# The first tiles of a stage multiplied at the end of the stage before it, in a two-block transformer kernel

## The chip, the cores and the metric

One core of one Trainium2 chip. The metric is the device time of one execution in microseconds, the median of the runs. TensorE (PE) multiplies, VectorE (DVE), ScalarE (ACT) and GpSimd (POOL) do the elementwise work, SyncE (SP) issues the transfers.

## The reference, cut to what matters

The kernel computes two model blocks over 512 positions of width 1024 in float32. Block one is an attention and RWKV mixer and an FFN of width 4096; block two has two layers, each a mixer and an FFN of width 2816. Each mixer ends in a projection `@ w_out`. What surrounds the change, for block two:

```python
def conv_ffn(h, w_in, conv_w, conv_b, w_out):
    u = h @ w_in
    u = lax.conv_general_dilated(u, conv_w[:, None, :], window_strides=(1,),
                                 padding=[(CONV_WIDTH - 1, 0)],
                                 dimension_numbers=('NWC', 'WIO', 'NWC'),
                                 feature_group_count=u.shape[-1]) + conv_b
    g, v = jnp.split(u, 2, axis=-1)
    return (jax.nn.silu(g) * v) @ w_out
...
        h = rms_norm_2(x, attn_norm[layer])
        if layer % 2 == 0:
            x = x + even_mixer(h, cos, sin, ...)
        else:
            x = x + odd_mixer(h, cos, sin, ...)
        h = rms_norm_2(x, ffn_norm[layer])
        x = x + conv_ffn(h, ffn_w_in[layer], ffn_conv_w[layer], ffn_conv_b[layer], ffn_w_out[layer])
```

## The kernel before, in words

All activations lie transposed, features on the 128 partitions and the 512 positions along the free axis, in eight slices of 128 features. A product of width 1024 is made tile by tile: a weight tile is 1024 x 128, loaded as 8 slices of 128 x 128. To keep float32 precision weights and activations are each cut into an upper and a lower part, and `three_passes` (L321) multiplies upper by upper, upper by lower and lower by upper: 24 matmuls of 128x128 by 128x512 for a tile (L326, L327, L328), summed in one PSUM bank.

One list, `plan` (L278), holds all weight tiles of the program in their order. Tile s passes SP's load into `raw` (two buffers, L286), ScalarE's upper part `whi` (`split_hi`, L302, or in a loop L813), GpSimd's lower part `wlo` (`split_lo`, L315, with L313 as the instruction) and TensorE's use. There are four buffers of `whi` and `wlo` (CUT = 4). ScalarE and GpSimd work AHEAD = 2 tiles ahead of TensorE: while a stage multiplies its tile m they split m + 2. Thus a stage ends with the first two tiles of the next one already split, and the next two loaded. `w_lo` counts tiles split, `w_used` tiles multiplied, `free` and `conved` the PSUM banks given back.

A stage is one Block (L149): all five engines meet in a barrier at its end and start the next stage together; GpSimd first clears the semaphores of the stage before (L158). The stages that the change touches, in the order of the program:
- `ffn` of block one, run twice with half of the width each (ch 0 and ch 1). The first stores its result in `f`, the second adds to it. Ch 0 begins with a norm (`Post`), ch 1 with nothing: the inputs `hi`, `lo` are the same, so its first tiles can be multiplied at once.
- `project_out` (L717) of each layer of block two: eight tiles; for each, VectorE adds to `xT` (L772), ScalarE makes the upper part of the next input and a square, VectorE the lower part (L775) and the sum of squares `acc` (L781).
- `ffn` of each layer of block two. It begins with `Ready` (L461): TensorE sums `acc` over the partitions (L393, 4 matmuls), VectorE and ScalarE form the reciprocal root, TensorE multiplies tile 0, spreads the root over the partitions (L402), and goes on with tile 1. VectorE scales each finished bank by the root (L963), so the products don't wait for it.
- `project` (L630) with four tiles (inputs of an indexer), begun by `Ready`; GpSimd scales the results (L650), TensorE and VectorE rotate three of them (`RotateTiles`, L603 and L610 to L614).
- `project` with 18 tiles, which begins with the indexer's own matmuls (L2107, L2113) and in which VectorE searches the largest scores.

In an `ffn` the up tiles use banks 0 to 3, four a turn, and the down tiles banks 4 and 5.

## Time and profile before

| | us |
|---|---|
| median of 3 runs (lowest, highest) | 2361.53 (2360.04, 2362.3) |
| profiled execution | 2364.71 |
| its span | 2362.9 |
| PE busy | 2201.6 (93%) |
| PEld busy (weight loads, beside PE) | 1765.5 (75%) |
| DVE busy | 1211.5 (51%) |
| ACT busy | 834.4 (35%) |
| POOL busy | 986.8 (42%) |
| lower parts of the weights, POOL L313, 347 times | 793.0 |

The table tells which engine is full on average: TensorE. The rest must be read by stretches. A row of the timeline gives start, duration, engine, line, operation, the tile written and those read, and in brackets how long the engine had been idle and which instruction released it. A release by "PEq L151" is the barrier between two stages. A matmul's printed duration (0.39 us) is longer than the distance to the next one, since they overlap; tiles are therefore measured from start to start.

### The profile page before, as it was taken

How to read it: one execution, taken by the hardware profiler on the slowest of the kernel's cores; microseconds unless marked ns; L12 is line 12 of the kernel's file. 1: busy time of each engine (PE TensorE's matmuls, PEld its weight loads, DVE VectorE, ACT ScalarE, POOL GpSimd, SP SyncE). 2: the span in 40 equal slices, each digit the busy share in tenths (PEclk: the TensorE clock that was granted, in tenths of full speed). 3: DMA queues.
4: the chain of work that ended last, by engine and by line, in shares of the span. 5: the costliest groups of instructions: out<-in, count | busy, mean ns of one | idle time of the engine just before them, and what ended most of it. 6: DMA issues, size and time to landing. Idle time of an engine off the chain costs nothing. (4 is left out here: it accounts for less than half of the span.)

```text
span 2362.9 us, 35241 instructions
## 1 busy us (share of the span) xinstructions
PE 2201.6 (93%) x13241; PEld 1765.5 (75%) x13241; DVE 1211.5 (51%) x1881; ACT 834.4 (35%) x1321; POOL 986.8 (42%) x515
## 2 busy tenths in 40 slices
PE   6995998699999999899879999999899899999998
PEld 4674986588888888777657788888676557888887
DVE  3336534677604772332663577731397633777601
ACT  3443222433313332332353333322323553333322
POOL 5231211244543444365563344444365514444442
PEclk8997999899999999999999999999999999999999
DMA  4220001223332333233102233333332003233332
GB/s 131 54 66 22 4 26 47 72 84 94 107 98 80 99 96 107 76 82 88 36 1 63 80 97 98 91 96 98 86 84 77 1 10 95 84 98 89 91 103 90
DMA packets 347229, 177.23 MB, mean 75 GB/s; under 512 B 20852, under 2 KB 344303, under 8 KB 347119
## 3 DMA queue, kind: packets, MB, share of 16 engines
q1 hardware_dynamic: 346620, 175.60, 26.0%
q8 instruction: 75, 1.23, 0.2%
q14 instruction: 36, 0.29, 0.0%
q10 hardware_dynamic: 210, 0.08, 0.0%
q0 software_dynamic: 288, 0.03, 0.0%
HBM read 173.57 MB, written 2.11 MB: 74 GB/s over the span
## 5 line engine op out<-in xcount | busy, mean ns | idle before, releaser
L313 POOL TENSOR_TENSOR wlo<-raw,whi 128x1024 fp32r<-128x1024 f32 (+3 forms) x347 | 793.0, 2289 | 1103.8 <-ACT whi L816 609.8
L326 PE MATMUL banks<-xhi,whi 128*128 128x512 f32 x1688 | 672.4, 398 | 6.0 <-DVE cb L974 3.9
L327 PE MATMUL banks<-xlo,whi 128*128 128x512 f32 x1688 | 661.9, 392 | 0.0
L328 PE MATMUL banks<-xhi,wlo 128*128 128x512 f32 x1688 | 661.7, 392 | 0.0
L326 PEld LDWEIGHTS banks<-xhi,whi 128*128 128x128 f32 x1688 | 320.2, 190 | 82.7 <-issue 12.9
L327 PEld LDWEIGHTS banks<-xlo,whi 128*128 128x128 f32 x1688 | 320.1, 190 | 69.0 <-issue 3.6
L328 PEld LDWEIGHTS banks<-xhi,wlo 128*128 128x128 f32 x1688 | 319.8, 189 | 67.6
L903 ACT ACTIVATE cb<-banks,conv 128x512 f32<-128x512 f32 x152 | 117.9, 778 | 446.6 <-DVE banks L963 446.6
L816 ACT ACTIVATE whi<-raw 128x1024 fp32r<-128x1024 f32 (+1 forms) x208 | 203.6, 988 | 172.1 <-PE banks L328 78.2
L326 PE MATMUL banks<-ghi,whi 128*128 128x512 f32 x608 | 236.6, 389 | 0.3 <-DVE glo L984 0.3
L327 PE MATMUL banks<-glo,whi 128*128 128x512 f32 x608 | 236.5, 389 | 0.0
L328 PE MATMUL banks<-ghi,wlo 128*128 128x512 f32 x608 | 236.5, 389 | 0.0
L963 DVE TENSOR_TENSOR banks<-banks,rs 128x512 f32<-128x512 f32 x152 | 106.2, 700 | 183.8 <-PE banks L328 166.5
L982 DVE CAST ghi<-gv 128x512 f32 (+1 forms) x76 | 168.4, 2216 | 9.0
L309 ACT ACTIVATE whi<-raw 128x1024 fp32r<-128x1024 f32 (+3 forms) x139 | 134.0, 970 | 47.3 <-PE banks L328 19.1
L326 PEld LDWEIGHTS banks<-ghi,whi 128*128 128x128 f32 x608 | 114.1, 188 | 24.3 <-DVE glo L984 0.7
L328 PEld LDWEIGHTS banks<-ghi,wlo 128*128 128x128 f32 x608 | 114.1, 188 | 23.8
L327 PEld LDWEIGHTS banks<-glo,whi 128*128 128x128 f32 x608 | 114.1, 188 | 23.6
L974 DVE SCALAR_TENSOR_TENSOR cb<-banks,conv,cb 128x510 f32<-128x510 f32 x152 | 113.8, 749 | 18.3 <-DVE cb L972 0.3
L972 DVE SCALAR_TENSOR_TENSOR cb<-banks,conv,cb 128x511 f32<-128x511 f32 x152 | 112.6, 741 | 3.8 <-ACT cb L903 3.8
L1005 DVE TENSOR_TENSOR xT<-banks,xT 128x512 f32 x16 | 11.1, 692 | 191.6 <-PE banks L328 191.6
L1054 POOL TENSOR_SCALAR ex<-ex,mx 128x128 f32<-128x128 f32 (+3 forms) x80 | 87.9, 1112 | 48.5 <-DVE mx L1116 34.1
(453 smaller groups left out, 2587.1 us busy)
## 6 DMA issues: line engine op xcount, KB each, us to landing
raw<-in_ffn_w_in_dram SPq DMA_DIRECT2D x88, 512.0 KB, 3.9
raw<-in_w_ffn_up_dram SPq DMA_DIRECT2D x64, 512.0 KB, 4.1
raw<-in_w_ffn_down_dram SPq DMA_DIRECT2D x32, 512.0 KB, 3.8
raw<-in_ev_w_in_dram SPq DMA_DIRECT2D x25, 512.0 KB, 4.0
raw<-in_ffn_w_out_dram SPq DMA_DIRECT2D x32, 384.0 KB, 3.5
raw<-in_ffn_w_out_dram SPq DMA_DIRECT2D x32, 320.0 KB, 3.2
raw<-in_od_w_in_dram SPq DMA_DIRECT2D x20, 512.0 KB, 3.9
raw<-in_w_in_dram SPq DMA_DIRECT2D x16, 512.0 KB, 3.8
```

The costliest lines, as they stand in the source:

```text
L309: w_hi.by(act.activation(whi[s % CUT][:, 0:n, :], raw[s % RAW][:, 0:n, :], ACT.Copy))
L313: return pool.tensor_tensor(wlo[c][:, 0:n, :], raw[b][:, 0:n, :], whi[c][:, 0:n, :].bitcast(F32), ALU.subtract)
L326: pe.matmul(acc, whi[b][:, k, :], hi(k), start=first and k == 0, stop=False)
L327: pe.matmul(acc, whi[b][:, k, :], lo(k), start=False, stop=False)
L328: mm = pe.matmul(acc, wlo[b][:, k, :], hi(k), start=False, stop=last and k == n - 1)
L816: act.activation(whi[s % CUT][:, 0:n, :], raw[s % RAW][:, 0:n, :], ACT.Copy).then_inc(w_hi.h, 1)
L903: act.activation(cb[j][:, :], bank[j][:, :], ACT.Identity, scale=conv[:, 2, bass.ds(c, 1)], bias=conv[:, 3, bass.ds(c, 1)])\
L963: dve.tensor_tensor(bank[j % 4][:, :], bank[j % 4][:, :], rs, ALU.mult).then_inc(scaled.h, 1)
L972: chain(dve.scalar_tensor_tensor(cb[j][:, 1:S], bank[j][:, 0:S - 1], conv[:, 1, bass.ds(c, 1)], cb[j][:, 1:S], ALU.mult, ALU.add))
L974: dve.scalar_tensor_tensor(cb[j][:, 2:S], bank[j][:, 0:S - 2], conv[:, 0, bass.ds(c, 1)], cb[j][:, 2:S], ALU.mult, ALU.add).then_inc(conve ...
L982: dve.tensor_copy(ghi[:, i * 2 + q, :], gv[q][:, :]).then_inc(upper.h, 1)
L1054: ins = pool.tensor_scalar(ex[u % 4][:, g, 0:w], ex[u % 4][:, g, 0:w], mx[u % 4][:, 2, g:g + 1], None, ALU.mult)
```

## The change: what it does

Five pairs of neighbouring stages are involved. The stage ahead gets a parameter `ahead` and the stage behind a parameter `done`. With `ahead=2` TensorE multiplies, after its own last tile, the first two tiles of the next stage into banks 0 and 1, before it goes to the barrier; with `done=2` the next stage begins with its third tile. Ffn ch 0 to ch 1, both `project_out` of block two to their `ffn`, and the first `ffn` of block two to the four-tile `project` do so with two tiles, the four-tile `project` to the 18-tile one with one tile. In the stage behind, the spread of the root comes after tile 2 in place of tile 0. Where the tiles ahead need the activation's lower part, a new signal `lowered` on VectorE's writes orders them. ScalarE's, GpSimd's and SP's programs keep their order, except that in the four-tile `project` GpSimd splits three tiles before it waits for the root, where it split one. A parameter `before` and a signal `moved` that nothing used are gone.

```diff
     def project(n, dst, lead=None, side=None, post=None, done=0, ahead=0):
...
-        lag = lead.SPREAD if lead else 0
+        lag = max(lead.SPREAD, done) if lead else 0
...
             def _(pe):
+                aside, done_lag = 0, lag if lead and done else 0
...
-                    if m >= tiles_:
+                    if m >= max(tiles_, done):
                         pe.wait_ge(w_lo.h, s + 1)
...
-                    if lead and m == lead.SPREAD:
+                    if lead and m == lag:
                         lead.pe_spread(pe)
-                    if m >= 1:
-                        side.pe(pe, scaled, m - 1)
-                side.pe(pe, scaled, n - 1)
+                    while m > done_lag and aside < m - ahead:
+                        side.pe(pe, scaled, aside)
+                        aside += 1
+                for j in range(ahead):
+                    pe.wait_ge(w_lo.h, s0 + n + j + 1)
+                    pe.wait_ge(free.h, n - 3 + j)
+                    three_passes(pe, bank[j][:, :], (s0 + n + j) % CUT, KD, lambda k: hi[:, k, :], lambda k: lo[:, k, :], True, True)\
+                        .then_inc(w_used.h, 1)
+                while aside < n:
+                    side.pe(pe, scaled, aside)
+                    aside += 1
...
+    def project_out(oT, scale, mixed=None, make_side=None, ahead=0):
...
+                for j in range(ahead):
+                    pe.wait_ge(w_lo.h, s0 + n + j + 1)
+                    pe.wait_ge(free.h, n - 3 + j)
+                    three_passes(pe, bank[j][:, :], (s0 + n + j) % CUT, KD, lambda k: feed["hi"][:, k, :], lambda k: feed["lo"][:, k, :], True, True,
+                                 lowered).then_inc(w_used.h, 1)
...
+    def ffn(w_up, ff, w_down, conv, first, pairs, parts, func, add, acc_to, make_lead=None, tail=None, done=0, ahead=0):
...
                     lead.pe_sums(pe)
-                    up(0, False, 0, 1)
+                    up(0, False, done, done + 1)
                     lead.pe_spread(pe)
-                    up(0, False, 1)
+                    up(0, False, done + 1)
                 else:
-                    up(0, False)
+                    up(0, False, done)
...
+                for j in range(ahead):
+                    pe.wait_ge(w_lo.h, end + j + 1)
+                    three_passes(pe, bank[j][:, :], (end + j) % CUT, KD, lambda k: hi[:, k, :], lambda k: lo[:, k, :], True, True,
+                                 lowered if tail else None).then_inc(w_used.h, 1)
...
-                        project(4, lambda m: to[m], lead=Ready(c1),
+                        project(4, lambda m: to[m], lead=Ready(c1), done=2, ahead=1,
...
-                    project(18, lambda m: dsts[m],
+                    project(18, lambda m: dsts[m], done=1,
...
-                ("sums",) if ch == 1 else None)
+                ("sums",) if ch == 1 else None, done=2 * ch, ahead=2 - 2 * ch)
...
-                project_out(oT, ("ffn_norm", KD * layer))
+                project_out(oT, ("ffn_norm", KD * layer), ahead=2)
...
-                ("feed", "attn_norm", KD) if layer == 0 else ("last", "final_norm"))
+                ("feed", "attn_norm", KD) if layer == 0 else ("last", "final_norm"), done=2, ahead=2 - 2 * layer)
```

TensorE's program before, from the end of the first `project_out` of block two into its `ffn`. L151 is the jump to the barrier, `whi_12` the second weight buffer, and a name behind "waits" can be that of an earlier use of the semaphore:

```order
L328 MATMUL banks<-hi,wlo_15 128x512
L151 UNCONDITIONAL_BRANCH
L853 UNCONDITIONAL_BRANCH [waits barrier_Pool_Activation_PE_DVE_SP_release]
L393 MATMUL banks<-cst,acc 128x1 x4
L326 MATMUL banks<-xhi,whi_12 128x512 [waits w_lo_22]
...
L402 MATMUL banks<-cst,st 128x128 [waits sq_114]
L402 MATMUL banks<-cst,st 128x128 x3
L326 MATMUL banks<-xhi,whi_13 128x512 [waits w_lo_22]
```

Tile 0 follows the barrier and the sums, the spread (L402) stands between tile 0 and tile 1. The same place after the change (here exped_91 is `lowered` and flipped_93 is `free`):

```order
L328 MATMUL banks<-hi,wlo_15 128x512
L326 MATMUL banks<-xhi,whi_12 128x512 [waits exped_91,flipped_93,w_lo_22]
...
L326 MATMUL banks<-xhi,whi_13 128x512 [waits exped_91,flipped_93,w_lo_22]
...
L151 UNCONDITIONAL_BRANCH
L865 UNCONDITIONAL_BRANCH [waits barrier_Pool_Activation_PE_DVE_SP_release]
L393 MATMUL banks<-cst,acc 128x1 x4
L326 MATMUL banks<-xhi,whi_14 128x512 [waits w_lo_22]
...
L402 MATMUL banks<-cst,st 128x128 [waits summed_115]
L402 MATMUL banks<-cst,st 128x128 x3
L326 MATMUL banks<-xhi,whi_11 128x512 [waits w_lo_22]
```

The tiles in `whi_12` and `whi_13` now stand ahead of the barrier, and the first tile behind it is that in `whi_14`.

GpSimd's program after the change, from the end of ffn ch 0 into ch 1 (before, it reads the same, with x28 in the row of L158):

```order
L313 TENSOR_TENSOR wlo_15<-raw_9,whi_11 128x1024 [waits w_hi_21]
L313 TENSOR_TENSOR wlo_16<-raw_10,whi_12 128x1024 [waits w_hi_21]
L151 UNCONDITIONAL_BRANCH
L155 UNCONDITIONAL_BRANCH [waits barrier_Pool_Activation_PE_DVE_SP_gather]
L158 ISA x29
L835 UNCONDITIONAL_BRANCH
L835 ISA
L313 TENSOR_TENSOR wlo_17<-raw_9,whi_13 128x1024 [waits w_hi_21]
```

The tile in `wlo_17`, the new stage's third, is cut behind the barrier and behind the clearing of the semaphores, in both kernels.

TensorE's program after the change, at the end of the four-tile `project` (pre_109 is `scaled`):

```order
L603 MATMUL banks<-iq,sw 128x512 [waits flipped_93,pre_109]
L603 MATMUL banks<-iq,sw 128x512 [waits pre_109]
L326 MATMUL banks<-xhi,whi_12 128x512 [waits sg1_110,w_lo_22]
...
L603 MATMUL banks<-ik,sw 128x512 [waits pre_109]
L151 UNCONDITIONAL_BRANCH
L660 UNCONDITIONAL_BRANCH [waits barrier_Pool_Activation_PE_DVE_SP_release]
L2123 MATMUL banks<-cst,ciw 128x128 x4
```

Before, each of the three rotations stood behind one tile; now two stand together, the tile done ahead (`whi_12`) follows them, and the third rotation is the last before the barrier.

## Rows read from the trace of the kernel before

**Rows 1.** The page, 40 slices of the span: TensorE's busy share in tenths.
```profile
PE   6995998699999999899879999999899899999998
```

**Rows 2.** TensorE's waits, whole span: waiter, releaser, us in total, times, longest.
```profile
PE banks L393 <- PEq L151: 20.1, 6, 4.4
...
PE banks L326 <- DVE lo L559: 15.1, 3, 8.6
...
PE banks L326 <- DVE cb L974: 3.9, 1, 3.9
PE banks L326 <- POOL wlo L313: 3.1, 1, 3.1
```

**Rows 3.** The timeline at seam 2, project_out to ffn, block two's first layer.
```profile
1299.89 0.39 PE L328 MATMUL banks<-hi,wlo 128*128 128x512 f32 x1
1303.86 1.84 PE L393 MATMUL banks<-cst,acc 128*128 128x1 f32 x8 [3.58 <-PEq L151]
1305.03 4.69 POOL L313 TENSOR_TENSOR wlo<-raw,whi 128x1024 fp32r<-128x1024 f32 x2 [4.69 <-ACT whi L816]
1313.30 1.05 PE L402 MATMUL banks<-cst,st 128*128 128x128 f32 x8
1314.11 0.48 PE L326 MATMUL banks<-xhi,whi 128*128 128x512 f32 x1
...
1330.54 0.39 PE L326 MATMUL banks<-xhi,whi 128*128 128x512 f32 x1
```

**Rows 4.** The timeline of TensorE at seam 5, project_out to ffn, second layer.
```profile
1982.12 0.39 PE L328 MATMUL banks<-hi,wlo 128*128 128x512 f32 x1
...
2012.96 0.39 PE L326 MATMUL banks<-xhi,whi 128*128 128x512 f32 x1
```

**Rows 5.** The timeline at seam 1, ffn ch 0 to ch 1.
```profile
714.39 0.39 PE L328 MATMUL banks<-ghi,wlo 128*128 128x512 f32 x1
714.94 0.69 DVE L1007 COPY f<-banks 128x512 f32 x1 [10.19 <-PE banks L328]
715.96 0.47 PE L326 MATMUL banks<-xhi,whi 128*128 128x512 f32 x1 [1.18 <-PEq L151]
718.07 2.40 POOL L313 TENSOR_TENSOR wlo<-raw,whi 128x1024 fp32r<-128x1024 f32 x1 [10.54 <-ACT whi L816]
...
729.94 0.75 DVE L974 SCALAR_TENSOR_TENSOR cb<-banks,conv,cb 128x510 f32<-128x510 f32 x1
...
737.84 0.39 PE L326 MATMUL banks<-xhi,whi 128*128 128x512 f32 x1
```

**Rows 6.** The timeline at seams 3 and 4, around the four-tile projection.
```profile
1667.60 0.39 PE L328 MATMUL banks<-ghi,wlo 128*128 128x512 f32 x1
1671.43 1.33 PE L393 MATMUL banks<-cst,acc 128*128 128x1 f32 x8 [3.44 <-PEq L151]
1672.62 2.36 POOL L313 TENSOR_TENSOR wlo<-raw,whi 128x1024 fp32r<-128x1024 f32 x1 [5.21 <-ACT whi L309]
...
1700.10 1.02 PE L603 MATMUL banks<-ik,sw 128*128 128x512 f32 x2
1703.91 0.63 PE L2107 MATMUL banks<-cst,ciw 128*128 128x128 f32 x4 [2.79 <-PEq L151]
```

**Rows 7.** TensorE in four stretches: length, busy (x), clock, DMA share, GB/s.
```profile
391.90:398.70 6.80, 3.09 (x7) 0.51 0.19 59
419.30:422.70 3.40, 3.40 (x9) 0.50 0.53 155
470.50:477.20 6.70, 5.07 (x12) 0.50 0.00 0
1303.40:1310.10 6.70, 6.24 (x19) 0.50 0.17 50
```

**Rows 8.** The timeline at the end of the 18-tile projection.
```profile
1807.59 1.95 DVE L2196 SCALAR_TENSOR_TENSOR ckv<-ckv,pcol,part 128x512 f32<-128x512 f32 x1
...
1817.83 2.84 PE L2229 MATMUL banks<-ckv,ukp 128*128 128x512 f32 x4 [2.32 <-PEq L151]
```

More of the change, by code:

```diff
@@ L628, in in_turn, with project @@
                     mm.then_inc(w_used.h, 1)
-    def project(n, dst, lead=None, side=None, post=None, before=None):
+    def project(n, dst, lead=None, side=None, post=None, done=0, ahead=0):
         s0 = state["s"]
@@ L697, in _ @@
                     act.wait_ge(w_used.h, s0 + m + 1)
-                    if before:
-                        before(act, m)
                     free.by(act.activation(dst(m), bank[m % 4][:, :], ACT.Copy))
@@ L715, in project @@
         state["s"] += n
-    def project_out(oT, scale, mixed=None, make_side=None):
+    def project_out(oT, scale, mixed=None, make_side=None, ahead=0):
         s0, n = state["s"], KD
@@ L721, in project_out @@
         to = xT if mixed is None else mixed
-        free, moved, uppered, squared, summed = (sig(x) for x in ("free", "moved", "uppered", "squared", "summed"))
+        free, uppered, lowered, squared, summed = (sig(x) for x in ("free", "uppered", "lowered", "squared", "summed"))
         with ExitStack() as ctx:
@@ L775, in _ @@
                         dve.scalar_tensor_tensor(feed["lo"][:, m - 1, :], xT[:, m - 1, :], col(scale[0], scale[1] + m - 1),
-                                                 feed["hi"][:, m - 1, :].bitcast(F32), ALU.mult, ALU.subtract)
+                                                 feed["hi"][:, m - 1, :].bitcast(F32), ALU.mult, ALU.subtract).then_inc(lowered.h, 1)
                     if m >= 2:
@@ L782, in project_out @@
         state["s"] += n
-    def ffn(w_up, ff, w_down, conv, first, pairs, parts, func, add, acc_to, make_lead=None, tail=None):
+    def ffn(w_up, ff, w_down, conv, first, pairs, parts, func, add, acc_to, make_lead=None, tail=None, done=0, ahead=0):
         hi, lo, rs, acc = feed["hi"], feed["lo"], feed["rs"], feed["acc"]
@@ L797, in ffn @@
             scaled, uppered, squared, summed = (sig(n) for n in ("scaled", "uppered", "squared", "summed"))
-            taken = sig("taken")
+            taken, lowered = sig("taken"), sig("lowered")
             chain0 = dve_chain.n
@@ L1010, in _ @@
                                 dve.scalar_tensor_tensor(lo[:, m, :], xT[:, m, :], pcol[:, bass.ds(m + (vec[tail[1]] + tail[2]), 1)],
-                                                         hi[:, m, :].bitcast(F32), ALU.mult, ALU.subtract)
+                                                         hi[:, m, :].bitcast(F32), ALU.mult, ALU.subtract).then_inc(lowered.h, 1)
                             if tail:
```

## The prediction

> **What bounds the kernel now.** I read the slices of the page first, for where TensorE is not full; then the waits of TensorE; then the timeline at the five seams the change touches; last the granted clock around idle stretches. The slices show TensorE at nine tenths or more in most of the span [rows 1]: the 24 matmuls of a weight tile follow each other without a hole. Three tiles fill 1314.11 to 1330.54, that is (16.43 - 0.1)/3 = 5.44 us a tile, the 0.1 being the slower first matmul after a stop [rows 3]. So the time can only change at the holes. The waits [rows 2] show that holes come in two kinds: TensorE held at a stage's start ("PEq L151", the barrier), and TensorE held for a split weight or activation tile.
>
> The seams, each measured from the start of the last matmul of the old stage to the start of the fifth tile of the new one (so that four tiles are inside):
> - seam 2, first output projection of block two into its FFN: 1299.89 to 1330.54 = 30.65 us [rows 3]. Inside stand a barrier after VectorE's and ScalarE's tail (hole 3.58), the sums, and a stretch at half clock.
> - seam 5, the same in the second layer: 1982.12 to 2012.96 = 30.84 us [rows 4].
> - seam 1, first FFN pass of block one into its second: 714.39 to 737.84 = 23.45 us [rows 5]; the hole is only 1.18 us and the four tiles (21.76) run at full clock.
> - seams 3 and 4, FFN into the four-tile projection and that into the 18-tile one: from 1667.60 to the first matmul of the 18-tile stage at 1703.91 = 36.31 us [rows 6].
>
> **What is added and what it waits for.** The extra tiles are the ones whose weights are already split, since ScalarE and GpSimd work two tiles ahead (AHEAD). Nobody works further ahead than before: the split of the third tile (index 2) still stands in the new stage, behind the barrier. Before, two tiles (10.88 us) ran over that split; now TensorE arrives at it at once. What it costs is in the rows: at seam 2 GpSimd starts at 1305.03, when ScalarE has done its half of the split, and needs 4.69/2 = 2.35 us for a tile, so tile 2 is ready 3.5 us after the stage's start (1303.86) [rows 3]. At seam 3 it is 1672.62 + 2.36 - 1671.43 = 3.55 [rows 6]. At seam 1 GpSimd starts only at 718.07, 2.11 us in: it clears 28 semaphores first (29 after the change); ready at 720.47, 4.5 us in [rows 5]. So the change hides a hole that was made by the old stage's tail and opens one made by the new stage's head, and the sum is the difference.
>
> The barrier with TensorE last: at seam 1 VectorE started 0.55 us after the start of the last matmul, and TensorE 0.33 us after VectorE's end (715.63 to 715.96) [rows 5]; 0.88 together. That is worked out from one seam; 0.6 to 1.2 would shift the total by about 1 us either way.
>
> Each seam after, from the same start, c being what the clock costs:
> - seam 2: two tiles 10.88, barrier 0.88, split 3.5 + 0.1 for the signal (the sums, 1.0 us, lie beside it), tile 2 5.54, the spread 0.81 (1313.30 to 1314.11 [rows 3]), tile 3 5.54 = 27.25 + c. Against 30.65: -3.4 + c.
> - seam 5: the same 27.25 + c against 30.84: -3.6 + c.
> - seam 1: 10.88 + 0.88 + 4.5 + 0.1 + 10.98 = 27.35 + c against 23.45: +3.9 + c. Here there was nothing to win but 1.2 us, and a wait of 4.5 us is put in.
> - seams 3 and 4: 10.88 + 0.88 + 3.55 + 0.1 + 5.54 + 0.81 + 5.54, two rotation matmuls of 0.5 us each (half of the row of 1.02, which is two passes), the tile done ahead 5.6, then the third rotation matmul and from its start the 3.81 us that it took before (1700.10 to 1703.91: VectorE's rotation is still behind it, uncovered [rows 6]) = 37.7 + c. The 18-tile stage then has one tile less, 5.54. So 32.2 + c against 36.31: -4.1 + c.
>
> Without c: +3.9 - 3.4 - 3.6 - 4.1 = -7.2 us.
>
> **The clock.** A TensorE that has stood still pays a second time. After the 3.1 us hole in block one's output projection the granted clock is 0.50 (1.2 GHz of 2.4) for 3.40 us of busy time, cost 1.7 us; after a 3.9 us hole 5.07 us busy, cost 2.5; after the 8.6 us hole 3.09 us busy, cost 1.5, the rest of the slow stretch having passed in the hole; at seam 2, hole and sums together, 6.24 us, cost 3.1 [rows 2, 7]. At seam 1 there is no slow stretch now: its 23.45 us are four tiles at 5.44 and the barrier [rows 5]. After the change seams 2, 3 and 5 have a hole of about 0.6 us, the sums (1.0) and a hole of 2.5: nearest is the 3.1 us hole, 1.7 each. (Of the old 3.1 I thus give back 1.4 at each; it is inside the -3.4, -3.6 and -4.1 already, since the 30.65, 30.84 and 36.31 hold the old slow stretches.) Seam 1 has a new hole of 5.2 us, between the 3.9 and the 8.6: 2.0. Together 3 x 1.7 + 2.0 = 7.1. Bounds of c: 0 at the low end, 3.4 at the high end (a slow stretch of 6.8 us with TensorE busy throughout).
>
> **Covers that I count at nothing.** The first tile done ahead reads as its last of eight slices the one that VectorE writes in the tail; the tail's whole hole is 3.58 us [rows 3], and that slice is asked for seven eighths into the tile, 4.8 us in. Banks 0 and 1 were freed long before. In the 18-tile stage ScalarE and GpSimd split tile 2 while tile 1 runs (5.44 us against the 3.5 that both engines took at seam 2 [rows 3]), a margin of nearly 2 us. VectorE begins tiles 0 and 1 no later than the new third tile ends; the fifth tile needs its bank back, and at seam 1 VectorE gives it at 729.94 + 0.75 = 730.69, 14.7 us into the stage [rows 5], while the new tile 3 ends 4.6 + 10.98 + c = 15.6 + c in: a thin cover of 0.9 us. VectorE's chain of the 18-tile stage ends at 1809.54 [rows 8] and the next stage starts at 1817.83, 0.33 us after all have arrived, so its slack is 8.0 us; these shrink by 5.5 to 2.5 [rows 8]. One semaphore more to clear is at most 2.11/28 = 0.08 us, at two stage starts.
>
> **Sum.** -7.2 + 7.1 = -0.1 us. The profiled execution would take 2364.7 us (span 2362.9 and 1.8 around it) less 0.1; the median of the runs lies 3.2 us below it, at 2361.5. I forecast 2361.4. A difference under 0.2% (4.7 us) can't be told from none here.
>
> **Rivals.**
> 1. The clock does not fall at the new holes of seams 2, 3 and 5: each is split by the sums into pieces of 0.6 and 2.5 us. Then only seam 1 pays: -7.2 + 2.0 = -5.2, 2356.3 us (2354.3 if it doesn't pay either). For it: the 1.18 us hole of seam 1 costs no clock today [rows 5]. Against it: a 3.1 us hole was followed by a slow stretch [rows 2, 7]. Chance 0.15. The Trainium skill (TensorE: Matmul & The Clock Gate, section "HAM oscillation — how this bites in real kernels") has a rule of thumb that only a wait above a certain length costs clock, and it sets that length above each of these pieces, so by it this rival would hold. The 3.1 us hole lies below that length too and was followed by the slow stretch, so the trace does not agree.
> 2. The clock falls for the whole long stretch at all four, c = 3.4: 13.6 - 7.2 = +6.4, 2367.9 us, slower. The place is seam 1 most of all, where +3.9 and 3.4 meet with nothing returned. It decides from a total c of 7.2 + 4.7 = 11.9 us on. For it: seams 2, 3 and 5 have the long stretch today, after holes no longer in total than the new ones. Chance 0.15.
> 3. Tile 2's weights are found split, and the holes close altogether: seam 2 becomes 10.88 + 0.88 + 1.0 + 5.44 + 0.81 + 5.44 = 24.45, -6.2; seam 5 -6.4; seams 3 and 4 -6.8 (37.7 less the 2.65 of waiting); seam 1 -0.8; together -20.2, 2341.3 us. Against it: ScalarE's and GpSimd's programs have the split of tile 2 behind the barrier as before. Chance 0.05.
> 4. VectorE's chain in the 18-tile stage becomes its end (its rotations wait in another order, or it stretches beside GpSimd): up to 5.5 of the 5.54 us of that tile are lost, 2367. Chance 0.05.
> The forecast with c between 1 and 2.9 a seam on average holds 0.60.
>
> **How the numbers follow.** Of the forecast's own 0.60, running from 2357 to 2366, nearly all is within 0.2%; some 0.05 falls out at the fast end and 0.02 at the slow end. Faster: 0.15 + 0.05 + 0.05 = 0.25. Slower: 0.12 of rival 2, 0.03 of rival 4 and 0.02 = 0.17. Same: 0.58. The range for 8 in 10 goes from 2354.5, at rival 1, to 2367.
>
> **What would show it.** Right: the barrier waits before the sums at seams 2, 3, 5 fall from about 3.5 to under 1 us, and new waits of TensorE for "POOL wlo" appear, 2.5 us at three seams and about 4.5 at seam 1, where a stretch at clock 0.5 is new; seam 4's 2.79 us hole stays. Wrong: no wait for "POOL wlo" at the stage starts (rival 3), or full clock behind them (rival 1).

## The result and the profile after

The changed kernel takes 2369.55 us (median of 6, 2367.58 to 2374.07) beside 2361.41 for the kernel before (6 runs, 2356.8 to 2362.3): ratio 1.0033, interval 1.0022 to 1.0043. It is slower by 8.1 us, more than the 4.7 us that can be told from no change. The forecast was 2361.4 and the range ended at 2367.0; both missed. A second comparison on another chip gave 2374.07 beside 2365.3, ratio 1.0037 (1.0022 to 1.0052).

In all that follows a "cut" is the making of the upper part (ScalarE) or the lower part (GpSimd, L313) of a weight tile, a "hole" is a stretch in which TensorE runs nothing, and a "slow stretch" is one in which its granted clock is at half. TensorE's waits in the changed kernel, whole span (waiter, releaser, us in total, times, longest); lines behind L313 have moved on by up to 16:

```profile
PE banks L326 <- POOL wlo L313: 16.0, 6, 4.9
...
PE banks L393 <- PEq L151: 11.5, 6, 5.4
...
PE banks L2245 <- PEq L151: 4.2, 1, 4.2
...
PE banks L2123 <- PEq L151: 2.5, 1, 2.5
```

Beside [rows 2]: the waits for the barrier ahead of the sums fell from 20.1 us to 11.5, and those for a cut tile rose from 3.1 us, once, to 16.0, six times. The four new waits for a cut are 12.6 us together, where the forecast had 2.5 us at three seams and about 4.5 at seam 1. The timeline at seam 1, all engines (start, duration, engine, line, operation, tiles, in brackets the idle time before and its releaser):

```profile
725.27 0.39 PE L328 MATMUL banks<-xhi,wlo 128*128 128x512 f32 x1
725.98 1.30 DVE L979 TENSOR_TENSOR banks<-banks,rs 128x512 f32<-128x512 f32 x2 [10.36 <-PEq L151]
726.03 2.00 ACT L828 ACTIVATE whi<-raw 128x1024 fp32r<-128x1024 f32 x2 [20.97 <-PEq L151]
728.17 4.66 POOL L313 TENSOR_TENSOR wlo<-raw,whi 128x1024 fp32r<-128x1024 f32 x2 [20.64 <-ACT whi L828]
...
730.56 0.80 PE L326 MATMUL banks<-xhi,whi 128*128 128x512 f32 x1 [4.90 <-POOL wlo L313]
```

GpSimd starts its cut 2.2 us into the stage and TensorE stands until the first of the two is done. The hole is 4.90 us where it was 1.18 [rows 5]. At seam 2 and at seam 5, TensorE alone:

```profile
1317.44 0.39 PE L328 MATMUL banks<-xhi,wlo 128*128 128x512 f32 x1
1318.15 1.02 PE L393 MATMUL banks<-cst,acc 128*128 128x1 f32 x8 [0.32 <-PEq L151]
1321.72 0.80 PE L326 MATMUL banks<-xhi,whi 128*128 128x512 f32 x1 [2.54 <-POOL wlo L313]
...
1329.91 1.05 PE L402 MATMUL banks<-cst,st 128*128 128x128 f32 x8
```
```profile
2004.08 0.80 PE L326 MATMUL banks<-xhi,whi 128*128 128x512 f32 x1 [2.54 <-POOL wlo L313]
```

The hole of 3.58 us ahead of the sums (the same at both seams before, [rows 3] show the first) is down to 0.32 at both, and one of 2.54 stands behind them. Its first matmul takes 0.80 us where one at full clock takes 0.48. The granted clock at these places, where 0.50 is 1.2 GHz of 2.4 (stretch, length, TensorE busy and its instructions, clock, DMA share, GB/s), in the order seam 1, seam 2, seam 3, behind the 18-tile stage, seam 5:

```profile
730.00:736.80 6.80, 6.24 (x15) 0.50 0.54 154
1320.50:1327.30 6.80, 5.58 (x13) 0.50 0.52 152
1689.10:1692.50 3.40, 3.40 (x9) 0.50 0.67 182
1822.20:1829.00 6.80, 5.38 (x7) 0.50 0.00 0
2003.10:2009.90 6.80, 5.83 (x14) 0.50 0.53 154
```

**The 18-tile stage.** It begins at 1712.79 and its successor at 1823.62, 110.83 us; before it was 1817.83 - 1703.91 = 113.92 [rows 6, 8]. It has one tile (5.54) less and is only 3.1 us shorter. Its end, TensorE and then VectorE:

```profile
1819.00 0.39 PE L328 MATMUL banks<-xhi,wlo 128*128 128x512 f32 x1
1823.62 2.05 PE L2245 MATMUL banks<-ckv,ukp 128*128 128x512 f32 x2 [4.24 <-PEq L151]
```
```profile
1818.94 3.35 DVE L2211 RECIPROCAL part<-sq 128x512 f32<-128x512 f32 x1
1822.33 0.75 DVE L2212 SCALAR_TENSOR_TENSOR ckv<-ckv,pcol,part 128x512 f32<-128x512 f32 x1
```

VectorE now ends last, at 1823.08, and TensorE waits 4.24 us where it waited 2.32. From the stage's first matmul VectorE's chain took 1809.54 - 1703.91 = 105.63 us before and 1823.08 - 1712.79 = 110.29 now. A large part of the difference is one group near its start, three additions of a 128x128 mask. In the kernel before, VectorE and GpSimd:

```profile
1713.90 2.70 DVE L2159 TENSOR_TENSOR score<-score,future 128x128 f32<-128x128 f32 x3
```
```profile
1713.54 2.50 POOL L313 TENSOR_TENSOR wlo<-raw,whi 128x1024 fp32r<-128x1024 f32 x1 [11.30 <-ACT whi L309]
1718.28 1.30 POOL L650 TENSOR_TENSOR cq<-cq,rs 128x512 f32<-128x512 f32 x1 [2.24 <-ACT cq L700]
```

and in the changed one:

```profile
1723.11 5.99 DVE L2175 TENSOR_TENSOR score<-score,future 128x128 f32<-128x128 f32 x3
1729.13 1.48 DVE L2183 MAX8 top<-score 128x8 f32<-128x256 f32 x3
```
```profile
1722.44 2.82 POOL L313 TENSOR_TENSOR wlo<-raw,whi 128x1024 fp32r<-128x1024 f32 x1 [17.47 <-ACT whi L309]
1725.23 1.34 POOL L650 TENSOR_TENSOR cq<-cq,rs 128x512 f32<-128x512 f32 x1
1726.52 2.43 POOL L313 TENSOR_TENSOR wlo<-raw,whi 128x1024 fp32r<-128x1024 f32 x1
1728.91 1.34 POOL L650 TENSOR_TENSOR cq<-cq,rs 128x512 f32<-128x512 f32 x1
```

Before, one GpSimd operation lay over the additions and they ended 0.56 us after it (1716.60 beside 1716.04). Now three GpSimd operations follow each other without a pause, and the additions end 0.15 us after the third (1729.10 beside 1728.95). Taken one by one, the three additions end at 1725.41, 1726.71 and 1729.10, and the three GpSimd operations at 1725.26, 1726.57 and 1728.95: each addition ends 0.14 or 0.15 us behind one of them. Before, the first waited in the same way (to 1716.20) and the other two took 0.28 us each. The order changed because tile 0's product is there from the start: its scaling (L650) stands ready at once, between the cuts, where it used to come later.

The same happens further on. VectorE rotates the first tiles of the stage (L610, L611, L614), and L614, which takes 0.69 us when it is alone, took 2.70 where it began beside a cut. For tile 0, before and after:

```profile
1729.87 0.69 DVE L614 TENSOR_TENSOR cq<-cq,rotated 128x512 f32<-128x512 f32 x1
```
```profile
1742.37 2.70 DVE L614 TENSOR_TENSOR cq<-cq,rotated 128x512 f32<-128x512 f32 x1
```

Which of these operations meet a cut differs between the two kernels, and the changed one meets more of them.

**Where the time stands.** TensorE's line cut at holes that every profile has, in us; the second column is a new profile of the kernel before (run b1_before_again below), the last the forecast's difference:

| from, to (times of the first profile) | before | before again | changed | forecast |
|---|---|---|---|---|
| 472.1 to 977.4, holds seam 1 | 505.23 | 505.24 | 511.92 | +5.9 |
| 1254.9 to 1703.9, holds seams 2 and 3 | 449.03 | 447.44 | 451.24 | +1.4 |
| 1703.9 to 1817.8, the 18-tile stage | 113.92 | 113.97 | 110.83 | -5.5 |
| 1817.8 to 1936.1 | 118.28 | 118.23 | 119.27 | 0 |
| 1936.1 to 2350.4, holds seam 5 | 414.29 | 412.91 | 413.33 | -1.9 |
| rest of the span, not touched | 762.2 | 763.8 | 761.8 | 0 |

A second profile of the changed kernel (run a1_changed_again) has 511.85, 451.16, 110.84, 119.28 and 413.28, all within 0.1 us of the first, and 765.7 in the rest: between these two executions only what the change leaves alone moved, by 4 us.

The +1.4 is seam 2's -1.7 and, for seams 3 and 4 with the tile done ahead still in, 37.7 + 1.7 - 36.31 = +3.1.

### The profile page after: what moved, and what is told of

Same layout as the page of the kernel before. It is cut to its first block and busy times, and to the rows that moved or that the text cites. A ratio compares the mean times of both kernels' runs of the same rounds, so it can differ in the third digit from the quotient of the medians.

```text
span 2368.4 us, 35252 instructions
## 1 busy us (share of the span) xinstructions
PE 2203.7 (93%) x13241; PEld 1764.7 (75%) x13241; DVE 1210.5 (51%) x1881; ACT 834.4 (35%) x1321; POOL 985.9 (42%) x515
## 5 line engine op out<-in xcount | busy, mean ns | idle before, releaser
L313 POOL TENSOR_TENSOR wlo<-raw,whi 128x1024 fp32r<-128x1024 f32 (+3 forms) x347 | 793.1, 2290 | 1125.0 <-ACT whi L828 612.9
L326 PE MATMUL banks<-xhi,whi 128*128 128x512 f32 x1688 | 673.1, 399 | 17.4 <-POOL wlo L313 12.6
L988 DVE SCALAR_TENSOR_TENSOR cb<-banks,conv,cb 128x511 f32<-128x511 f32 x152 | 112.6, 741 | 12.6 <-ACT cb L919 12.6
```

The costliest lines, as they stand in the source:

```text
L313: return pool.tensor_tensor(wlo[c][:, 0:n, :], raw[b][:, 0:n, :], whi[c][:, 0:n, :].bitcast(F32), ALU.subtract)
L326: pe.matmul(acc, whi[b][:, k, :], hi(k), start=first and k == 0, stop=False)
L988: chain(dve.scalar_tensor_tensor(cb[j][:, 1:S], bank[j][:, 0:S - 1], conv[:, 1, bass.ds(c, 1)], cb[j][:, 1:S], ALU.mult, ALU.add))
```

## The experiments

Each is an edit of the changed kernel unless said otherwise. Ratios are to the kernel before, timed on the same chip; profile segments are against the table's first column.

**e1_seam1_only and e2_without_seam1: is it seam 1?**

```diff
 e1: tiles ahead at seam 1 alone
-    project_out(oT, ("ffn_norm", KD * layer), ahead=2)
+    project_out(oT, ("ffn_norm", KD * layer))
-    done=2, ahead=2 - 2 * layer)
+    )
-    project(4, ..., lead=Ready(c1), done=2, ahead=1,
+    project(4, ..., lead=Ready(c1),
-    project(18, ..., done=1,
+    project(18, ...,
 e2: everything but seam 1
-    done=2 * ch, ahead=2 - 2 * ch)
+    done=0, ahead=0)
```

> Only seam 1 (FFN ch 0 to ch 1) has its two tiles ahead; the other seams are as before. Theory (the change loses at seam 1: TensorE waits 4.9 us for GpSimd's cut of the third tile and then runs 6.8 us at half clock): in the profile the second FFN pass starts its fifth tile 6 to 7 us later than before, and all behind it is shifted by that; timed +5 to +7.5 us against before. Rival (seam 1 is neutral, the loss lies at the later seams): within 1 us of before.

Measured: 2370.58 (11 runs) beside 2364.48, ratio 1.0024 (1.0015 to 1.0033), 6.1 us slower, as expected; its segment with seam 1 is 5.64 longer. The fifth tile starts 5.2 us later than before (28.68 us for 23.45), not 6 to 7: the hole is 4.90 us again, but the slow stretch behind it is 3.4 us long in this profile, not 6.8.

> The changed kernel with seam 1 undone, seams 2 to 5 kept. Theory: the timed result falls by 6 to 7 us from the changed kernel's, to -1 to +2 us against before, since seams 2 and 5 return 1 us each, seam 3 with 4 returns 2.4 and gives 2.4 back in the 18-tile stage and 1 more by the clock. Rival (the loss of 8 us lies in seams 2 to 5): still +5 us or more.

Measured: 2366.14 (12 runs, one of them a stray 5605.41) beside 2364.48, ratio 1.0008 (1.0000 to 1.0017), 1.7 us. That is inside the expected -1 to +2, and the interval reaches 1.0000. So seam 1 carries most of the loss, and the other four together don't gain, where the forecast had them at -7.2 - 3.9 + 3 x 1.7 = -6.0.

**e3_without_seam4: what is the tile ahead at seam 4 worth?**

```diff
-    project(4, ..., lead=Ready(c1), done=2, ahead=1,
+    project(4, ..., lead=Ready(c1), done=2,
-    project(18, ..., done=1,
+    project(18, ...,
```

> The changed kernel without the one tile ahead at seam 4 (four-tile projection to 18-tile one). Theory (VectorE's chain ends the 18-tile stage once TensorE has one tile less): the hole at that stage's end falls from 4.2 to 2.3 us, the half-clock stretch behind it from 6.8 to 3.4 us, and the time does not rise though a tile of work goes back: -1 us against the changed kernel, so +4 to +7 against before. Rival (TensorE's chain ends the stage in both): the tile ahead is worth its cover, and without it the kernel is 2 us slower or more than the changed one.

Measured: 2373.87 (5 runs) beside 2364.48, ratio 1.0042 (1.0029 to 1.0055). The hole at the end of the 18-tile stage is 2.32 us and the slow stretch behind it 3.4, as expected, but the gain did not come: the kernel is 9.4 us over before, where the changed one is 8.1 and 8.8 over. That is less than the 2 us of the rival too, and the intervals overlap. What ate the gain stands at the other end of the stage. TensorE at the end of the four-tile stage:

```profile
1706.80 0.59 PE L603 MATMUL banks<-ik,sw 128*128 128x512 f32 x1
1713.09 1.09 PE L2123 MATMUL banks<-cst,ciw 128*128 128x128 f32 x4 [5.70 <-PEq L151]
```

With two tiles gone to the stage before and none put in, nothing is left to multiply beside the rotations, and the hole is 5.70 us against 2.79 [rows 6] and 2.45 with the tile. The clock is at half for 6.8 us after it, and the 18-tile stage takes 114.68.

**e4_mask_early: take VectorE's additions out of GpSimd's way.**

```diff
+                if x == 8:
+                    dve.wait_ge(self.got.h, 80)
+                    dve.wait_ge(self.added.h, 9)
+                    for t, _ in tiles_:
+                        y = self.score[:, t - 1, t * P:(t + 1) * P]
+                        ins = dve.tensor_tensor(y, y, self.future, ALU.add)
+                    chain(ins)
...
-            dve.wait_ge(self.got.h, 80)
             dve.wait_ge(self.added.h, len(self.order))
-            for n, _ in tiles_:
-                x = self.score[:, n - 1, n * P:(n + 1) * P]
-                ins = dve.tensor_tensor(x, x, self.future, ALU.add)
-            chain(ins)
```

> The changed kernel, with VectorE's three additions of the mask (128x128 each) in the 18-tile stage moved ahead of GpSimd's first cut of that stage. Theory (they took 5.99 us in place of 2.70 because GpSimd's cuts, now back to back, hold what both engines share): the three additions take under 1.5 us in all, VectorE's chain ends 2.5 to 4 us earlier, the hole at the stage's end falls to 2.3 to 3 us, and the kernel gains 1.5 to 3 us on the changed one. Rival (the additions are late because TensorE's first matmuls ran at half clock): they still take 5 us or more wherever they stand, and nothing is gained.

Measured: 2369.76 (10 runs) beside 2364.48, ratio 1.0021 (1.0012 to 1.0031): 5.3 us over before where the changed kernel is 8.1 and 8.8 over, which fits the expected 1.5 to 3, though the intervals overlap. VectorE, its last operation of the chain at the stage's end, and then GpSimd:

```profile
1724.81 0.70 DVE L2176 TENSOR_TENSOR score<-score,future 128x128 f32<-128x128 f32 x3
1725.54 4.42 DVE L2170 SCALAR_TENSOR_TENSOR score<-part,iwt,score 128x512 f32<-128x512 f32 x3
1730.00 1.48 DVE L2185 MAX8 top<-score 128x8 f32<-128x256 f32 x3
...
1816.14 1.80 DVE L2214 SCALAR_TENSOR_TENSOR ckv<-ckv,pcol,part 128x512 f32<-128x512 f32 x1
```
```profile
1726.62 2.79 POOL L313 TENSOR_TENSOR wlo<-raw,whi 128x1024 fp32r<-128x1024 f32 x1 [17.47 <-ACT whi L309]
1729.38 1.73 POOL L650 TENSOR_TENSOR cq<-cq,rs 128x512 f32<-128x512 f32 x1
```

Alone the three additions take 0.70 us, so 5.3 of the 5.99 were waiting. But the operations behind them (L2170, 2.46 us before) now meet the cut and take 4.42. The stage is 109.27 in place of 110.83 (its end hole is 2.32 again) and the slow stretch after it 3.4 us in place of 6.8. The meeting was moved, not removed. Yet the chain ends 1817.94 - 1716.97 = 100.97 us into the stage, 9.3 us sooner than in the changed kernel and not the expected 2.5 to 4, since with the additions moved the later operations fall elsewhere between GpSimd's and wait less (L611 and L614 together 12.6 us, 18.0 in the changed kernel). So the meetings set the chain's length, but what one of them costs can't be read from its own row. The rival (additions late because of the clock) is out: they took 0.70 us.

**a1_changed_again, e5_split_ahead, e6_split_and_mask, e8_seam1_split_ahead: cut further ahead as well.** In e5 ScalarE and GpSimd cut as many further tiles before the barrier as TensorE has multiplied ahead, so that the third tile is ready when the new stage starts. The core of the edit (in `project`; `project_out` and `ffn` likewise):

```diff
 GpSimd
-                    split_lo(pool, s0 + m + AHEAD)
+                    if m >= done:
+                        split_lo(pool, s0 + m + AHEAD)
...
+                for j in range(ahead):
+                    split_lo(pool, s0 + n + AHEAD + j)
 ScalarE
-                    if m >= AHEAD or not lead:
+                    if m >= AHEAD or not lead and m >= done:
                         split_hi(act, s0 + m + AHEAD)
...
+                for j in range(ahead):
+                    split_hi(act, s0 + n + AHEAD + j)
```

e6 is e5 with e4's edit, e8 is e5's for seam 1 alone and nothing ahead at the others.

> The changed kernel itself, on the same chip as the next three. It should come out 5 to 9 us slower than before, as in its first timing (8.1 us), and give the number that the others are held against.

> The changed kernel, with ScalarE's and GpSimd's cuts of as many further tiles as TensorE multiplies ahead moved in front of the barrier too, at all five seams (the four cut buffers suffice). Theory: the waits of TensorE for GpSimd's cut behind the barriers (4.9, 2.5, 2.6, 2.5 us) go, and with them the slow stretches there (3.0, 2.6, 1.6, 2.6 us), 20 to 22 us in all; 12 to 16 us faster than before. Rival (the cut buffers or ScalarE's place in its queue make TensorE wait elsewhere, or the clock falls anyhow at the barrier and the sums): the waits come back at the fifth tile or the slow stretches stay, and under half of it is gained, 2 to 5 us faster than before.

> The kernel with all cuts ahead, and VectorE's three mask additions ahead of GpSimd's first cut of the 18-tile stage. Theory: another 1 to 3 us on the one without it, since VectorE's chain no longer ends that stage: hole there 2.3 us in place of 4.2. Rival (VectorE's chain ends it still, since the stage before starts it in the same way): hole 4 us, no gain.

> Only seam 1 has its two tiles ahead, and there the cuts of the third and fourth tile stand ahead of the barrier as well; all else is as before. Theory: TensorE starts the third tile 0.7 to 1 us after its last matmul, no slow stretch follows, and the kernel is within 1.5 us of before, where the same seam without the cuts ahead cost 6 us. Rival (the tiles ahead cost by themselves, as through the loop's end or the bank's return): still 3 us or more slower than before.

Measured, beside 2365.3: a1 2374.07 (10 runs), 1.0037 (1.0022 to 1.0052); e5 2346.39 (6 runs), 0.9923 (0.9903 to 0.9942); e6 2346.63 (6 runs), 0.9924 (0.9906 to 0.9942); e8 2364.84 (12 runs), 1.0000 (0.9989 to 1.0011). Seam 1 and seam 2 in e5, TensorE:

```profile
726.37 0.39 PE L328 MATMUL banks<-xhi,wlo 128*128 128x512 f32 x1
...
727.08 0.47 PE L326 MATMUL banks<-xhi,whi 128*128 128x512 f32 x1 [0.33 <-PEq L151]
```
```profile
1311.96 0.39 PE L328 MATMUL banks<-xhi,wlo 128*128 128x512 f32 x1
1312.67 1.02 PE L393 MATMUL banks<-cst,acc 128*128 128x1 f32 x8 [0.32 <-PEq L151]
1313.56 0.48 PE L326 MATMUL banks<-xhi,whi 128*128 128x512 f32 x1
```

All that is left of a seam is 0.71 us for the barrier and 0.89 for the sums; no stretch at half clock follows at any of the five. The segments against before, in the table's order: -0.83, -7.51, -6.53, +0.04, -6.29, and +2.1 in the rest, which the edits leave alone. This version beats both kernels, by 18.9 us the one before, more than the 12 to 16 expected. e8 says that seam 1 has no more to give than its 1.18 us hole, since all that followed it is gone there and the kernel is as fast as before. e6 gains nothing on e5, against both its theory and its rival, which took the hole in e5 for one of 4 us: it is 2.32. In e5 VectorE ends at 1802.14, before TensorE's last matmul (start 1802.27), so its chain no longer sets the end.

**b1_before_again, e9_seam4_split_ahead, e7_split_ahead_without_seam4: what was left.** b1 is the kernel before, unedited. e9 is the changed kernel with the cut ahead at seam 4 only; e7 is e5 with e3's edit.

```diff
 e9, in project, GpSimd's part (ScalarE's likewise); nothing in project_out and ffn
-                    split_lo(pool, s0 + m + AHEAD)
+                    if lead or m >= done:
+                        split_lo(pool, s0 + m + AHEAD)
...
+                for j in range(ahead):
+                    split_lo(pool, s0 + n + AHEAD + j)
```

> The kernel before once more, for its profile. Its first profile (2364.71 us) lay 3.3 us above its median, that of the changed kernel only 0.7 above; so the two profiles differ by 5.5 us where the times differ by 8.1. If that profile was a somewhat slow execution, this one lies nearer its median, with the same segments and fewer or shorter stretches at half clock away from the seams: TensorE at half clock in less than 160.5 us in sum. If the 2.6 us are a real cost that the profile hides, this profile reads about 2364.7 again and the median 2361 to 2364.

Measured: 2364.92 (11 runs) beside 2364.67, ratio 1.0005 (0.9996 to 1.0014); profile 2363.38, now below its median. TensorE's clock is at half for 154.3 us in sum, as expected less than the 160.5 of the first profile. In the new profile two slow stretches are half as long as in the first one, at seam 3 and behind the 2.43 us hole at 1936:

```profile
1673.40:1676.80 3.40, 3.40 (x12) 0.51 0.12 27
1676.80:1680.20 3.40, 3.40 (x16) 0.99 0.59 154
1936.30:1939.70 3.40, 3.40 (x10) 0.50 0.00 0
1939.70:1943.10 3.40, 3.40 (x16) 1.00 0.00 0
```

against, in the first profile:

```profile
1672.00:1678.80 6.80, 6.80 (x20) 0.50 0.35 90
1934.80:1941.60 6.80, 5.49 (x13) 0.50 0.00 0
```

They make the -1.59 and -1.38 in the table. The 3.44 us hole at seam 3 is the same in both. In e1 and e8, which leave seam 3 alone, that stretch is 3.4 us too: three profiles of four have the short one, and the forecast was made from the fourth. The second stretch is 3.4 in b1, e4, e7 and e8 and 6.8 in the other nine.

> The changed kernel, with the cut of one further tile made before the barrier at seam 4 only (ScalarE and GpSimd, for the 18-tile stage); the other seams as changed. Theory (in the 18-tile stage VectorE's mask additions meet GpSimd's cuts and pay 3.3 us, and TensorE waits for that chain): the additions are back near 2.7 us, the 18-tile stage is 2 to 3 us shorter than the changed kernel's 110.8, the slow stretch behind it 3.4 us long in place of 6.8, and the time is 2 to 4 us under the changed kernel's, ratio about 1.0022 in place of 1.0035. Rival (the loss comes from the order of the tiles, not from the meeting): the stage stays at 110.8 and the ratio at 1.0035.

Measured: 2369.87 (8 runs) beside 2364.67, ratio 1.0027 (1.0017 to 1.0038). VectorE at the start and the end of the stage:

```profile
1726.02 2.70 DVE L2180 TENSOR_TENSOR score<-score,future 128x128 f32<-128x128 f32 x3
```
```profile
1818.53 1.97 DVE L2217 SCALAR_TENSOR_TENSOR ckv<-ckv,pcol,part 128x512 f32<-128x512 f32 x1
```

GpSimd beside the additions has now one cut, then a pause of 1.06 us:

```profile
1725.34 2.84 POOL L313 TENSOR_TENSOR wlo<-raw,whi 128x1024 fp32r<-128x1024 f32 x1
1729.23 1.30 POOL L651 TENSOR_TENSOR cq<-cq,rs 128x512 f32<-128x512 f32 x1 [1.06 <-ACT cq L710]
```

The additions are back at 2.70, the chain from the stage's first matmul (1714.86) to 1820.50 is 105.64 as before, the hole at the end 2.32, the slow stretch 3.4, and the stage 108.48: 5.44 less than before, the whole tile. The rival (order of the tiles) is out. That the chain has the length of before is the sum of several differences, not of the additions alone: one operation ahead of them took 1.60 us for 0.75, and L614 of tile 0 1.77 for 0.69, while later ones waited less. In the profiles e9 is 3.4 us shorter than the changed kernel over these two segments; timed, the excess over before is 5.2 us against 8.1 and 8.8, though the intervals of the two ratios overlap.

> The version with the cuts ahead at all seams, but with no tile ahead at seam 4. By the sum of the segments the tile ahead at seam 4 together with its cut returned 6.5 us in the 18-tile stage for 5.5 added in the four-tile one, so leaving it out should cost 1 us plus what the clock takes behind a longer hole there (1.5 to 3): 2349 to 2350, ratio 0.9935 to 0.9940 in place of 0.9923. Rival: that tile is worth 4 to 5 us as in the changed kernel, ratio 0.9945.

Measured: 2354.51 (5 runs) beside 2364.67, ratio 0.9961 (0.9947 to 0.9975). Both expectations were too low: with the cuts ahead the tile at seam 4 is worth 18.9 - 10.2 = 8.7 us, the two timed on different chips. The barrier wait at seam 4 is 5.7 us again, as in e3, a 6.8 us stretch at half clock is back behind it, and the stage is 114.63 against 107.39 in e5, while the part before it is only 2.1 shorter. The two profiles differ by 8.8, of which the segments give 4.7 and parts that no edit touches the rest, so the size is less sure than the sign.

## Why the prediction was wrong, step by step

Two steps of the prediction failed: the price of the clock behind the new holes ("nearest is the 3.1 us hole"), and the cover of VectorE's chain in the 18-tile stage ("these shrink by 5.5 to 2.5"). A third term rested on a profile that was not typical.

- **Places and sizes of the holes: right.** Forecast behind seams 2 and 5: barrier 0.88, split 3.6. Measured 0.71 and 3.57. Seam 3: 3.65. Seam 1: 5.48 forecast, 730.56 - 725.27 = 5.29 measured. Without c the forecast for seam 2 (27.25) is met to 0.2 us. The hole at seam 4, said to stay at 2.79, is 2.45.
- **The clock, c: mis-sized at three of four seams.** Seam 1 is 30.10 us long, from 714.39 to the start of the fifth tile at 744.49; two tiles, 5.29 and 10.98 leave 2.95 for c, forecast 2.0. At seam 2 the tile behind the hole takes 8.19 us for 5.54 (1321.72 to the spread at 1329.91): c is 2.65, forecast 1.7; at seam 5 8.33 us (2004.08 to 2012.41), c 2.8. Seam 3 (1688.57 to 1695.75): 7.18 for 5.54, 1.64, forecast 1.7. The step that failed: "nearest is the 3.1 us hole". Hole, sums and hole together were followed by the long stretch, with TensorE busy in 5.6 to 6.2 of its 6.8 us. Sum: 10.0 for 7.1. At seam 1 the six profiles with the 4.90 us hole have 28.7 us (e1, slow stretch 3.4) and 29.6 to 30.1 us (the other five, 6.8), so the forecast's 2.0 lies between and the first profile is the usual case. Rival 2 was right in kind, and its 3.4 each was the bound that it was said to be. Its reason, that the old holes were no longer than the new ones, misreads the rows: 3.58 and 3.44 us against 0.6 + 2.5 forecast and 0.32 + 2.54 measured. The long stretch came even so.
- **"These shrink by 5.5 to 2.5": failed.** This is rival 4, given 0.05; of its two reasons it was the second, stretching beside GpSimd. VectorE's slack of 8.0 us would have held if its chain had kept its length; it grew by 4.66, so it ended 2.2 us too late. Operation by operation: +0.3 from a later start, +3.3 in the mask additions, +3.5 in the rotations (L610, L611 and L614), -1.25 in the first comparison with the threshold (L2201, 1.27 us for 2.52) and -1.2 in the last operation (L2212, 0.75 for 1.95). The growth is thus the difference between meetings with GpSimd that came in and meetings that went away. That these set the chain's length is shown by e4 (100.97) and e9 (105.64), which change the order and nothing that VectorE computes; that the mask additions are the part that matters isn't. The cost is 2.4 us in the stage and 1.0 behind it, where the hole grew from 2.32 to 4.24 and the slow stretch from 3.4 to 6.8 us. That the longer hole is the reason for the 1.0 isn't shown: e4 has the 2.32 us hole and a stretch of 3.4, and this segment is 0.95 longer than before all the same, with a second slow stretch later in it (at 1877.5). I had set the cover by a subtraction of lengths, without asking what GpSimd does beside VectorE in the new order.
- **The credit at seam 3 was taken from a long stretch.** -4.1 rests on 36.31 us, in which the clock was at half for 6.8 us; the other profiles that leave this seam alone have 3.4 there, which makes it 34.7. The seam itself came out as said: 1712.79 - 1673.33 = 39.46 for 39.4. Against the usual case it returned 0.8 us and not 2.4. One profile could not tell that.
- **The sum again.** Forecast -0.1. Add 0.8 at seam 1, 0.8 at seam 2, 0.9 at seam 5, 2.4 and 1.0 for the 18-tile stage: +5.8, which is what the segments of the two first profiles differ by. With the two short stretches of b1, 1.6 and 1.4, it is 8.8, beside 8.1 and 8.8 timed. That the medians go with b1's pattern fits, but isn't shown: it rests on four profiles with seam 3 untouched, and the untouched parts of the span vary too (761.8 to 765.7 us).
- **Rivals 1 and 3.** Rival 1 fell: every new hole was followed by a stretch at half clock. The rule of thumb of the Trainium skill that the prediction set beside it (TensorE: Matmul & The Clock Gate, section "HAM oscillation — how this bites in real kernels") would have had seams 2, 3 and 5 pay nothing, and they paid 2.65, 1.64 and 2.8 us; the traces do not agree with it. Rival 3 fell for this kernel, as the reason given against it said, and its arithmetic came true in e5: segments of -0.8 (seam 1), -14.0 (seams 2 to 4) and -6.3 (seam 5) where it had -0.8, -13.0 and -6.4, and -18.9 us timed for -20.2. Part of that match is luck: e5's profile has no slow stretch at seam 4, while e6's, whose program is the same up to there, has one of 6.8 us and -11.8 for seams 2 to 4.

## What to carry to other kernels

Moving one engine's work over a barrier moves the wait to the next thing that still stands behind the barrier: if TensorE goes two tiles ahead, those who feed it must go two tiles ahead too, and only then is there something to win (here +8.1 us without, -18.9 with). A cover worked out by subtracting lengths holds only while the covered chain meets the same neighbours; look at what GpSimd does beside VectorE in the new order. Read more than one profile of the kernel before when a term rests on a stretch at half clock. And leave a seam alone where there is little to win: at seam 1 it was 1.18 us, and the tiles ahead put a hole of 4.90 in its place.

## What the runs showed of the hardware

- Three additions of 128x128 with both inputs in SBUF took 0.70 us alone, 2.70 beside one GpSimd operation, and 5.99 beside three in a row, each held one ending 0.14 or 0.15 us after a GpSimd operation. VectorE wasn't slowed in proportion; it stood. In the same stage L610, with one input in PSUM, took 0.67 to 0.69 us every time, and L614, with both in SBUF, 0.69 to 2.70. The Trainium skill has this (SBUF — State Buffer, section "SBUF: two separate sides"): of a VectorE operation with two inputs in SBUF and a GpSimd operation that reads SBUF, the one that starts first has a shared pair of ports for its whole instruction, and the other one waits. The trace agrees.
- The same hole is not followed by the same slow stretch. Behind the 3.44 us hole at seam 3 it was 6.8 us once and 3.4 three times. Behind the 2.45 us hole at seam 4 there was none in e5, 6.8 us in e6, whose program is the same up to there, and 3.4 in the changed kernel and in e9. Behind the 4.90 us hole at seam 1 it was 6.8 us in five profiles and 3.4 in one (e1). What decides it stays open.
- The barrier itself, with TensorE last and the next work ready, cost TensorE 0.71 us at seams 1, 2, 3 and 5 in e5 (start of the last matmul to the next instruction). What an engine does first behind it comes on top: at seam 1 of the changed kernel GpSimd clears 29 semaphores, one each 0.07 us, and starts its cut at 728.17, 2.2 us into the stage, while ScalarE's half of that tile ended at 727.09; at seam 2 it clears 7, and waits for ScalarE until 1.2 us in. A kernel that clears them only after the first cut was not tried.
